# Three up tiles of a feed-forward stage with other column splits: 172, 258 and 86, or 512 and 8 in place of 344

## The reference, cut to what matters

```python
def conv_ffn(hn, buf, p):
    t = hn.shape[1]
    u = hn @ p['w_up']
    full = jnp.concatenate([buf.astype(u.dtype), u], axis=1)
    y = p['conv_b']
    for j in range(CONV_W):
        y = y + p['conv_w'][j] * full[:, j:j + t]
    a, g = jnp.split(y, 2, axis=-1)
    return (jax.nn.silu(a) * g) @ p['w_down'], full[:, -(CONV_W - 1):]
```

## Time and profile before

| | |
|---|---|
| median of 3 executions | 2427.32 us (2424.94 to 2427.94) |
| the profiled execution, its own time | 2431.48 us |
| span of the profiled execution, first to last instruction | 2429.7 us |
| mean granted TensorE clock | 0.989 of full speed |
| PE busy | 2320.2 us, 95% |
| PEld busy | 2168.3 us, 89% |
| DVE busy | 1611.9 us, 66% |
| ACT busy | 996.2 us, 41% |
| POOL busy | 798.7 us, 33% |

### The profile page before, as it was taken

The page is one execution under the profiler, slowest core; times in us unless marked ns, Lnnn a source line. Parts: engine busy times, 40 slices in busy tenths (PEclk is TensorE's granted clock), DMA queues, the critical chain, the costliest instruction groups (busy, mean ns, idle before and its releaser), DMA issues. The chain is left out here.

```text
span 2429.7 us, 46021 instructions
## 1 busy us (share of the span) xinstructions
PE 2320.2 (95%) x18425; PEld 2168.3 (89%) x18425; DVE 1611.9 (66%) x2711; ACT 996.2 (41%) x2072; POOL 798.7 (33%) x1019
## 2 busy tenths in 40 slices
PE   7899999899999999899999899999999999999999
PEld 6788888888888888888888799998999999999999
DVE  5568676767767686776778515417876677667667
ACT  6455555656555555655432402114322222222221
POOL 1034251524334251524344214442322232232222
PEclk9999999999999999999999999999999999999999
DMA  6213022221213021221598523111111111111112
GB/s 268 88 37 106 27 72 79 62 80 48 87 52 98 29 91 58 62 89 45 203 340 318 225 87 114 44 56 39 44 44 52 44 44 44 52 44 48 46 47 94
DMA packets 75343, 213.18 MB, mean 88 GB/s; under 512 B 15738, under 2 KB 24186, under 8 KB 75130
## 3 DMA queue, kind: packets, MB, share of 16 engines
q1 hardware_dynamic: 73978, 206.05, 25.1%
q10 hardware_dynamic: 1152, 4.19, 0.4%
HBM read 175.49 MB, written 26.26 MB: 83 GB/s over the span
## 5 line engine op out<-in xcount | busy, mean ns | idle before, releaser
L170 PE MATMUL h_G<-xn_hi,h_w_hi 128*128 128x344 f32 x1392 | 467.8, 336 | 8.4 <-ACT h_d_oraw L858 5.0
L170 PE MATMUL h_G<-xn_hi,h_w_lo 128*128 128x344 f32 x1392 | 445.2, 320 | 0.0
L170 PE MATMUL h_G<-xn_lo,h_w_hi 128*128 128x344 f32 x1392 | 444.9, 320 | 0.0
L2299 POOL TENSOR_TENSOR h_w_lo<-h_w_raw,h_w_hi 128x1024 fp32r<-128x1024 f32 x88 | 212.9, 2420 | 397.4 <-ACT h_w_hi L2070 388.1
L2240 PE MATMUL t_ps<-hn_hi,h_w_hi 128*128 128x344 f32 x1032 | 331.1, 321 | 0.0
L2240 PE MATMUL t_ps<-hn_lo,h_w_hi 128*128 128x344 f32 x1032 | 330.3, 320 | 0.0
L2240 PE MATMUL t_ps<-hn_hi,h_w_lo 128*128 128x344 f32 x1032 | 330.2, 320 | 0.0
L1120 POOL TENSOR_TENSOR h_w_lo<-h_w_raw,h_w_hi 128x1024 fp32r<-128x1024 f32 x58 | 146.3, 2523 | 493.8 <-ACT h_w_hi L738 448.3
L170 PEld LDWEIGHTS h_G<-xn_hi,h_w_hi 128*128 128x128 f32 x1392 | 263.8, 190 | 45.8 <-issue 17.1
L170 PEld LDWEIGHTS h_G<-xn_lo,h_w_hi 128*128 128x128 f32 x1392 | 262.3, 188 | 4.8 <-issue 0.7
L170 PEld LDWEIGHTS h_G<-xn_hi,h_w_lo 128*128 128x128 f32 x1392 | 262.2, 188 | 0.0
(11 more groups left out here) (367 smaller groups left out, 5540.1 us busy)
## 6 DMA issues: line engine op xcount, KB each, us to landing
h_w_raw<-in_w_in SPq DMA_DIRECT2D x72, 512.0 KB, 4.4
h_w_raw<-in_w_ffn SPq DMA_DIRECT2D x66, 512.0 KB, 3.6
h_d_ada_w<-in_w_ada SPq DMA_DIRECT2D x32, 512.0 KB, 5.0
g_kp<-in_cache_k SPq DMA_DIRECT2D x32, 512.0 KB, 7.0
g_vp<-in_cache_v SPq DMA_DIRECT2D x32, 512.0 KB, 5.4
h_w_raw<-in_w_mix SPq DMA_DIRECT2D x24, 512.0 KB, 3.7
x<-in_xT SPq DMA_DIRECT2D x16, 516.0 KB, 7.3
n_ada_w<-in_w_ada SPq DMA_DIRECT2D x16, 512.0 KB, 12.3
```

Of the source, the lines that this page charges most:

```text
L170: ins = eng.matmul(out, w[:, k * P:(k + 1) * P], x[:, k, columns], start=(k == 0 and n == 0), stop=(k == n_k - 1 and n == 2))
L2299: pool.tensor_tensor(wlo[buf(n)][:, :], raw[n % 2][:, :], whi[buf(n)][:, :].bitcast(F32), ALU.subtract).then_inc(w_lo.sem, 1)
```

## The change

Three of the 44 up tiles get other column ranges; everything else stays. In tile 20 each piece of 344 columns is made as two halves of 172 (first all 24 products of columns 0 to 172, then all 24 of 172 to 344, into the same bank). In tile 23 each piece is made as 258 and 86 columns. In tile 26 the three pieces are 512, 512 and 8 columns wide in place of 344 each, and ScalarE reads them in these widths. The same weight blocks are loaded again for the second part of a split piece.

```diff
+WIDE_TILE, SPLIT_TILES = 26, {20: TH // 2, 23: 3 * TH // 4}
+
+
+def up_columns(t, j):
+
+    return slice(512 * j, min(512 * (j + 1), NT)) if t == WIDE_TILE else cols(j)
...
-                act.activation(u[s][:, 2 + j * TH:2 + (j + 1) * TH], ffn_bank(t, 0, j), ACT.Copy).then_inc(up_free.sem, 1)
+                at = up_columns(t, j)
+                act.activation(u[s][:, 2 + at.start:2 + at.stop], ps[:, FFN_AT[t, 0, j] % BANKS, 0:at.stop - at.start], ACT.Copy).then_inc(up_free.sem, 1)
...
-                w = buf(MIX_TILES + t)
-                for k in range(KT):
-                    if t == 0:
-                        pe.wait_ge(n_hi.sem, n_hi.at(j * KT + k + 1, 0))
-                        pe.wait_ge(n_lo.sem, n_lo.at(j * KT + k + 1, 0))
-                    for q, (wp, xp) in enumerate(((whi, hh), (whi, hl), (wlo, hh))):
-                        ins = pe.matmul(ffn_bank(t, 0, j), wp[w][:, k * P:(k + 1) * P], xp[:, k, cols(j)],
-                                        start=(k == 0 and q == 0), stop=(k == KT - 1 and q == 2))
+                w, at = buf(MIX_TILES + t), up_columns(t, j)
+                n, cut = at.stop - at.start, SPLIT_TILES.get(t, 0)
+                for c0, c1 in ((0, cut), (cut, n)) if cut else ((0, n),):
+                    for k in range(KT):
+                        if t == 0:
+                            pe.wait_ge(n_hi.sem, n_hi.at(j * KT + k + 1, 0))
+                            pe.wait_ge(n_lo.sem, n_lo.at(j * KT + k + 1, 0))
+                        for q, (wp, xp) in enumerate(((whi, hh), (whi, hl), (wlo, hh))):
+                            ins = pe.matmul(ps[:, FFN_AT[t, 0, j] % BANKS, c0:c1], wp[w][:, k * P:(k + 1) * P], xp[:, k, at.start + c0:at.start + c1],
+                                            start=(k == 0 and q == 0), stop=(k == KT - 1 and q == 2))
```

## The result

The changed kernel takes 2439.5 us (median of 4 executions, 2437.18 to 2442.8), the kernel before in the same session 2427.63 us (4 executions). The ratio is 1.0048 with a 95% interval of 1.0027 to 1.0068: 0.5% slower, by 6.6 to 16.5 us. The forecast was 2439.7 us.

What follows compares the result with a forecast made beforehand. The prediction took TensorE, busy for 95% of the span, as the bound. Tiles 20, 23 and 26 and a shorter wait, 4.80 + 5.49 + 2.27 - 0.19 = +12.4 us on 2427.32, gave 2439.7 us; range 2435 to 2469.

Steps and rivals of the forecast that it cites:

- TensorE alone decides here: In the three changed up tiles TensorE waits for nobody, so its gain or loss goes into the end almost one to one.
- The load floor of 112 ns: Products 8, 86 and 172 columns wide start 112 ns apart, held by the weight load; 2436 to 2445 us, chance 0.52.
- The 14.1 ns that stay fixed above the columns' own time: Wide products cost columns at 2.4 GHz plus 14.1 ns whatever the width: 121.6 ns for 258, 227.4 for 512.
- The fall of the clock: After tile 26's 8-column piece, half speed for 3.4 us would cost 1.6 us; one chance in four, left out of the sum.
- The -0.19 us for ScalarE's shorter last read: ScalarE's last read of tile 26 shrinks to 8 columns, cutting TensorE's 0.38 us loss in the down tile behind by 0.19 us.
- the 0.38 read from the earlier trace: In the down tile behind tile 20, one product starts 0.54 us after another instead of 0.157, so 0.38 us are lost.
- Narrow products at the plain float32 rate: Rival: narrow float32r products in tiles 20 and 23 take four cycles a column; sum +39.8 us, 2467 us, chance 0.31.
- No floor, the load hides anyway: Rival: loads run ahead, as for a pair of 9-column products 0.02 to 0.03 us apart; +2.1 us, 2429.4, chance 0.12.
- The sum of 12.4 us: Tile 20 +4.80, tile 23 +5.49, tile 26 +2.27, ScalarE's shorter last read -0.19, together +12.4 us.

## Why the prediction came out right, point by point

- **TensorE alone decides here.** Shown: 40 tiles of halves cost 189.0 us, 4.73 us each, and one cost 4.72.
- **The load floor of 112 ns.** Right, and its cause is now shown and not only argued: half the weight columns, 58 ns; 2-byte weights, no floor down to 33 ns. Tile 20 came to 16.05 us for 16.13, tile 23 to 16.64 for 16.82; what is short of the sum is mostly the second product of each narrow run, which comes 0.03 to 0.07 us behind the first and not 0.112.
- **The 14.1 ns that stay fixed above the columns' own time** were the step that was mis-sized. The excess grows with the width: a product takes 3.7 + 0.446 ns a column. At 258 columns, near the floor, 121 ns were measured for 121.6, so tile 23 did not notice; at 512 columns it is 232.7 ns and not 227.4, and tile 26 took 13.77 us and not 13.60. The inference came from plain float32 streams, which take two array cycles a column; they show no excess at 344 columns either, so they could say nothing of how 14.1 ns would grow.
- **The fall of the clock**, put at one in four and left out of the sum, came in all three kernels with one such tile, and 21 times in the kernel with 40. The odds were too low. Its price of 1.6 us was right where nothing absorbs it (+1.62 with the 8 columns first). Behind tile 26 the down tile grew by 1.12 us only, since TensorE at half speed came too late to wait for VectorE at all: 72 x 157.4 ns and 1.62 us make 12.95 us, and 12.96 were measured.
- **The -0.19 us for ScalarE's shorter last read** was therefore not to be seen behind tile 26. Where no fall covers it, it was right in kind and too small: -0.30 us with 8 columns last, -0.23 with 72. And a wait costs 0.5 us and not the 0.38 read from the earlier trace rows, since the product behind it comes late too.
- **Narrow products at the plain float32 rate** are excluded: from 8 to 240 columns the median distance is 111 to 113 ns.
- **No floor, the load hides anyway** is excluded for a stream, but the row that spoke for it was rightly read: behind a wide product two narrow ones start 0.03 us apart, and the third 0.11 us later. With bfloat16 operands the load does hide in a whole stream. The 81 ns that the Trainium skill gives a sustained stream of 128 columns ("TensorE: Matmul & The Clock Gate", "Back-to-back issue gap") fit neither type here: float32r comes at 112 ns, bfloat16 of 86 and 172 columns at 41 and 77.

The sum of 12.4 us against 13.5 in the windows is 8% short: the narrow runs took 0.4 us less than it says, the wide ones 0.3 more, the clock and the wait 1.3 more. That the medians moved by 11.9 and not 13.5 us lies inside their interval. So it is luck that the forecast meets the median to 0.2 us: a term left out and the scatter of four executions, 5.6 us wide, cancel.

## What to carry to other kernels

Price a matmul stream as the larger of two lines, both taken from the kernel's own trace: the columns streamed, and the load of a new weight block; with float32r and 128 weight columns they meet at some 243 columns, and above that the way in which the columns are split hardly matters (0.05 us a tile in the one case tried), below it every further product costs a whole load. Beware of a short run of products with almost no columns: it is busy in the profile and can still be followed by microseconds at half clock. And a small wait that a chain shows again and again is worth more than such widths: one reordered read, off the busiest engine, gave 0.46%.

## What the runs showed of the hardware that was not expected

- Beyond 3.7 ns a product, a column of float32r costs 0.446 ns at full clock, 7% more than 1 / 2.4 ns, and at half clock exactly 1 / 1.2 (344 columns in 287 ns in the down tile behind tile 26, 512 in 427 ns in the kernel with 8 columns first). The cause stays open: a narrower load beside the product changes nothing, a 2-byte type with a step of two takes a third to a half of the excess away.
- The weight load of float32r goes with the number of weight columns: 112 ns for 128, 58 for 64, at most 42 for 32. That of bfloat16 takes at most 33 ns for 128.
- The granted clock fell 21 times behind 40 pieces of 24 products of 8 columns, 14 times behind 40 of 24 columns, and never behind 40 of 72 columns nor in 40 tiles of 172, although TensorE was busy throughout the up tiles in each. Of the falls, 18 of 21 and 14 of 14 came with the first tile of a pair.
